# Opening of a fused transformer kernel: two value units multiplied before the shift is known

## The reference, cut to what matters

```python
ada = jax.nn.silu(c) @ w_ada[l] + b_ada[l]
sh1, sc1, g1, sh2, sc2, g2 = [a[:, None, :] for a in jnp.split(ada, 6, axis=-1)]
h = x * (1.0 + sc1) + sh1
qa, ka, va, qb, kb, vb = jnp.split(h @ w_in, AB_SPLITS, axis=-1)
```

## Time and profile before

| | |
|---|---|
| median of 3 runs | 1231.37 us |
| the profiled execution | 1228.85 us |
| its span | 1227.2 us |
| PE busy | 1188.8 us (97%) |
| DVE busy | 673.6 us (55%) |
| ACT busy | 503.5 us (41%) |
| chain that ended last | PE 79%, DVE 8%, DMA 8%, ACT 3% |
| DMA in the first 31 us (the first of 40 slices) | 370 GB/s |

### The profile page before, as it was taken

The page is one execution under the profiler, slowest core; times in us unless marked ns, Lnnn a source line. Parts: engine busy times, 40 slices in busy tenths (PEclk is TensorE's granted clock), DMA queues, the critical chain, the costliest instruction groups (busy, mean ns, idle before and its releaser), DMA issues.

```text
span 1227.2 us, 16442 instructions
## 1 busy us (share of the span) xinstructions
PE 1188.8 (97%) x6522; PEld 816.1 (66%) x6522; DVE 673.6 (55%) x1206; ACT 503.5 (41%) x779; POOL 53.6 (4%) x103
## 2 busy tenths in 40 slices
PE   6999999999999999999999999999999999999997
PEld 2697688888889878888878786455444444544436
DVE  5689979887889787864476685112111111111126
ACT  1579563434565576344448384111111111111125
POOL 0100001000010000010001100000000000000000
PEclk9999999999999999999999999999999999999999
DMA  9996868888846555856567779999999999999991
GB/s 370 391 350 269 315 235 323 333 311 300 315 162 244 187 214 202 304 192 216 186 234 247 265 309 415 418 425 423 426 425 428 424 426 425 427 423 426 425 421 43
DMA packets 50987, 394.98 MB, mean 322 GB/s; under 512 B 6673, under 2 KB 8913, under 8 KB 11378
## 3 DMA queue, kind: packets, MB, share of 16 engines
q1 hardware_dynamic: 39618, 337.18, 68.6%
q0 software_dynamic: 9072, 53.92, 12.3%
q10 hardware_dynamic: 2240, 3.10, 0.9%
HBM read 390.68 MB, written 3.49 MB: 321 GB/s over the span
## 4 chain that ended last, share of the span: by engine, by line
PE 79%; DVE 8%; DMA 8%; ACT 3%; issue 1%; SPq 1%; DVEq 0%; ACTq 0%
PE psum L1400 16%; PE psum L770 10%; PE psum L773 10%; PE psum L777 10%; PE psum L1443 7%; DMA slabs<-in_w 5%; PE psum L1332 4%; PE psum L843 2%; PE psum L847 2%; PE psum L845 2%; DMA staged<-in_ada 2%; PE psum L1340 2%; DVE w_parts L2151 2%; PE psum L1095 1%; PE psum L1107 1%; PE psum L1086 1%
## 5 line engine op out<-in xcount | busy, mean ns | idle before, releaser
L2151 DVE TENSOR_TENSOR w_parts<-w_raw,w_parts 128x2048 fp32r<-128x2048 f32 x106 | 241.7, 2287 | 62.4 <-ACT w_parts L1533 62.3
L1533 ACT ACTIVATE w_parts<-w_raw 128x2048 fp32r<-128x2048 f32 x106 | 202.0, 1911 | 70.6 <-DMA w_raw<-in_units 70.5
L1400 PE MATMUL psum<-slabs,arena 128*64 128x512 f32 x768 | 223.2, 593 | 2.4 <-DMA w_odd_late<-in_w 1.8
L770 PE MATMUL psum<-w_parts,h_parts 128*128 128x512 f32 x392 | 155.2, 396 | 3.7 <-ACT h_parts L1533 1.9
L773 PE MATMUL psum<-w_parts,h_parts 128*128 128x512 f32 x392 | 153.0, 390 | 0.0
L1533 ACT ACTIVATE arena<-psum 128x512 f32<-128x512 f32 (+1 forms) x59 | 29.9, 509 | 295.3 <-PE psum L1419 141.7
L1400 PEld LDWEIGHTS psum<-slabs,arena 128*64 128x64 f32 x768 | 71.3, 137 | 112.7 <-issue 106.8
L777 PE MATMUL psum<-w_parts,h_parts 128*128 128x512 f32 x392 | 105.3, 390 | 0.6 <-DVE h_parts L2329 0.6
L2134 DVE CUSTOM_DVE_ANT_0 aring<-aring,cb 128x1024 f32<-128x1024 f32 x80 | 94.5, 1218 | 1.2 <-DMA aring<-in_ada 1.2
L770 PEld LDWEIGHTS psum<-w_parts,h_parts 128*128 128x128 f32 x392 | 73.6, 188 | 20.3 <-issue 2.9
L1400 PE MATMUL psum<-w_odd,arena 128*64 128x512 f32 x192 | 85.1, 593 | 0.4 <-DMA slabs<-in_w 0.4
(11 more groups left out here) (338 smaller groups left out, 1932.1 us busy)
## 6 DMA issues: line engine op xcount, KB each, us to landing
w_raw<-in_units SPq DMA_DIRECT2D x110, 1024.0 KB, 5.0
slabs<-in_w SPq DMA_DIRECT2D x52, 1024.0 KB, 15.4
slabs<-in_w SPq DMA_DIRECT2D x22, 2048.0 KB, 21.7
aring<-in_ada POOLq DMA_DIRECT2D x40, 1024.0 KB, 5.6
arena<-in_w SPq DMA_DIRECT2D x16, 2048.0 KB, 20.7
w_odd<-in_w SPq DMA_DIRECT2D x16, 2048.0 KB, 19.8
w_odd<-in_w SPq DMA_DIRECT2D x24, 1024.0 KB, 25.5
staged<-in_ada SPq DMA_DIRECT2D x8, 1024.0 KB, 18.7
```

The source lines that it names most:

```text
L770: mm(psum[:, bank, :], high(tile, tok), w_hi(k)[:, col:col + 512], start=first and bank not in begun, stop=False, skip_group_check=True)
L1400: ins = nc.tensor.matmul(psum[s * CAP:(s + 1) * CAP, w, :], xe_t[:, kt, s * CAP:(s + 1) * CAP], up_weights(w, s, b, kt), start=kt == 0, st ...
L1533: return nc.scalar.activation(out_ap, in_ap, func, **kw)
L2151: v.tensor_tensor(w_lo(k), raw(k), w_hi(k).bitcast(F32), ALU.subtract).then_inc(w_split, 1)
```

## The change

The order of the conditioning pieces becomes 4, 5, 6, 2, 7, 3, 0, 1: the scales of kt 0 to 3 first, then scale and shift of kt 4 to 7, and the shifts of kt 0 to 3 last (`LATE_SHIFT` = 4). Units 0 and 1 are multiplied with `x * scale` alone. Their missing part is made when the shifts are there: `shift_products` multiplies the shift, copied to 32 columns, with units 0 and 1, one tile of features on each quarter of the array's columns, into PSUM banks 4 and 5; ACT and DVE split that into two rounded parts (`shift_rows`), and `shift_sums` adds the parts to the four value banks through a matrix of ones. The other half of `h` (`h_hi`, `h_lo` of kt 0 to 3) is made late too (`shifted_h`, `first_low`), from `x_first` with the shift as a bias.

Query/key unit 4 is worked on in two halves of its tiles (`first_heads`): kt 4 to 7 before the shift products, kt 0 to 3 behind them. It and unit 5 write to PSUM banks 6 and 7 instead of 0 and 1. Units 0 and 1 lie in buffers of their own (`w1_odd`, `v_second`), since they are needed until the end of the opening. Some semaphores take over a second use, with their later counts raised.

The diff, without the semaphores' second uses:

```diff
@@ -82,9 +82,10 @@
 RMS = ("mix", "ple_proj", "ffn", "gate", "final")
 GAINS = ("g_mix", "g_ple_proj", "g_ffn", "g_ple", "g_final")
 
-CONSTS, LATER = 2 * 16, 6 * 16
-
-ADA_ORDER = (4, 0, 5, 1, 6, 2, 7, 3) + tuple(range(8, 48))
+CONSTS, LATER = 2 * 16, 5 * 16
+
+ADA_ORDER = (4, 5, 6, 2, 7, 3, 0, 1) + tuple(range(8, 48))
+LATE_SHIFT = 4
 STAGED = 8
 ADA_PIECES = 48
 
...
@@ -282,6 +283,10 @@
 
         w2_at = [arena[:], at("w2_odd", 0, [P, 8192])[:]]
 
+        first_v = [w1_odd[:], at("v_second", 178, [P, UNIT])[:]]
+        shift_rows = at("shift_rows", 136, [P, 2, 2, 512], F32R)
+        shift_ones = at("shift_ones", 144, [P, P], F32R)
+
         def slab(which, s, b):
 
...
@@ -531,18 +544,31 @@
-            for i in range(4):
-                stage(2 * i)
-                if i < 3:
-                    tiles = slice(2 * i, 2 * i + 2 if i < 2 else KT)
-                    sp.dma_start(x_first[:, tiles, :], a["x_t"][:, tiles, :]).then_inc(staged_in[2 * i + 1], 16)
-                stage(2 * i + 1)
-                load_unit(i)
+            stage(0)
+            sp.dma_start(x_first[:, 0:2, :], a["x_t"][:, 0:2, :]).then_inc(x_first_in[0], 16)
+            load_unit(0)
+            stage(1)
+            sp.dma_start(x_first[:, 2:4, :], a["x_t"][:, 2:4, :]).then_inc(x_first_in[1], 16)
+            load_unit(1)
+            stage(2)
+            stage(3)
+            sp.dma_start(x_first[:, 4:KT, :], a["x_t"][:, 4:KT, :]).then_inc(x_first_in[2], 16)
+            load_unit(2)
+            stage(4)
+            stage(5)
+            load_unit(3)
             load_unit(4)
...
-            small_loads(((lam_in[:], a["lam_in"]), (bias[:, 16, :], a["causal"]), (w_forget[:], a["w_forget"]),
+            stage(6)
+            stage(7)
+            load_unit(5)
+            load_unit(6)
+            sp.dma_start(lam_in[:], a["lam_in"]).then_inc(lam_arrived, 16)
+            load_unit(7)
...
@@ -694,6 +720,7 @@
 
 
             pool.wait_ge(bias_copied, 16)
+            pool.wait_ge(w_loaded[0], 32)
             bands(0, 4)
             pieces(8, 22)
             pool.wait_ge(unit_done, WO_AT + 4)
...
@@ -802,11 +829,55 @@
                         for c in range(2):
                             col = 1024 * s + 512 * c
                             ins = mm(psum[:, 2 * t + c, :], x_first[:, 2 * i + s, t * P:(t + 1) * P],
-                                     raw(V_AT + i)[:, col:col + 512], start=i == 0 and s == 0, stop=i == 3 and s == 1,
+                                     raw(V_AT + i)[:, col:col + 512], start=i == 0 and s == 0, stop=False,
                                      skip_group_check=True)
-                    if i == 3 and t == 0:
-                        ins.then_inc(v_half, 1)
                 ins.then_inc(unit_done, 1)
+
+            def first_heads(tiles):
+
+                k = QK_AT
+                begins, ends = tiles[0] == LATE_SHIFT, tiles[-1] == LATE_SHIFT - 1
+                made = lambda kt: (kt - LATE_SHIFT) % KT + 1
+                at_ = lambda kt, s: slice(kt * 256 + s * P, kt * 256 + (s + 1) * P)
+                pe.wait_ge(w_hi_ready, split_no(k))
+                for n, kt in enumerate(tiles):
+                    pe.wait_ge(h_high, made(kt))
+                    for s in range(2):
+                        mm(half(6, s), w_hi(k)[:, at_(kt, s)], h_hi[:, kt, :], start=begins and n == 0 and s == 0, stop=False,
+                           skip_group_check=True)
+                for kt in tiles:
+                    pe.wait_ge(h_low, made(kt))
+                    for s in range(2):
+                        mm(half(6, s), w_hi(k)[:, at_(kt, s)], h_lo[:, kt, :], start=False, stop=False, skip_group_check=True)
+                weights(k)
+                for kt in tiles:
+                    for s in range(2):
+                        ins = mm(half(6, s), w_lo(k)[:, at_(kt, s)], h_hi[:, kt, :], start=False,
+                                 stop=ends and kt == tiles[-1], skip_group_check=True)
+                if ends:
+                    ins.then_inc(unit_done, 1)
+
+            def shift_products():
+
+                pe.wait_ge(ada_done, STAGED)
+                for c in range(2):
+                    for kt in range(LATE_SHIFT):
+                        ins = mm(psum[32 * kt:32 * kt + 32, 4 + c, :], ada[:, 0, kt:kt + 1].to_broadcast([P, 32]),
+                                 raw(V_AT + kt // 2)[:, kt % 2 * 1024 + c * 512:kt % 2 * 1024 + c * 512 + 512],
+                                 start=True, stop=True, skip_group_check=True)
+                    ins.then_inc(shift_mm, 1)
+
+            def shift_sums():
+
+                pe.wait_ge(shift_high, 2)
+                for t in range(TT):
+                    for c in range(2):
+                        for part in range(2):
+                            if part and t == 0:
+                                pe.wait_ge(shift_low, shift_low_from + c + 1)
+                            ins = mm(psum[:, 2 * t + c, :], shift_ones[:], shift_rows[:, part, c, :], start=False, stop=part == 1,
+                                     skip_group_check=True)
+                    ins.then_inc(v_half, 1)
 
             def to_values(i, t):
                 return from_h(LAYER_UNITS + V_AT + i, i // 2, t, 2 * t + i % 2, 1)
...
@@ -1184,6 +1258,10 @@
                 if layer == 0:
                     for i in range(4):
                         first_values(i)
+                    first_heads((4, 5, 6, 7))
+                    shift_products()
+                    first_heads((0, 1, 2, 3))
+                    shift_sums()
                     pe.wait_ge(consts_in, CONSTS)
                 else:
                     to_values(0, 0)
...
@@ -1567,7 +1645,15 @@
             act.wait_ge(rows_mm, 1)
             A(cb[:], psum[:, 5:7, :].rearrange("p c n -> p (c n)"), ACT.Silu).then_inc(silu_c, 1)
 
+            def first_scaled(p):
+                act.wait_ge(x_first_in[p], 16)
+                act.wait_ge(scale_ready, p + 1)
+                for kt in (2 * p, 2 * p + 1):
+
+                    A(x_first[:, kt, :], x_first[:, kt, :], Cp, scale=small[:, kt:kt + 1]).then_inc(h_first, 1)
+
...
+            def shifted_h(p):
+                act.wait_ge(ada_done, 7 + p)
+                for kt in (2 * p, 2 * p + 1):
+                    act.wait_ge(h_first, kt + 1)
+                    A(h_hi[:, kt, :], x_first[:, kt, :], Id, bias=ada[:, 0, kt:kt + 1]).then_inc(h_high, 1)
+
+            first_scaled(0)
+            for dst, src in ((cst[:], a["consts"]), (added_in[:], a["added"])):
+                act.dma_start(dst, src).then_inc(consts_in, 16)
+            first_scaled(1)
+            act.wait_ge(bias_row, 1)
+            act.dma_start(scratch, added_in[:].unsqueeze(1).to_broadcast([16, COPIES, 384])).then_inc(bias_copied, 16)
+            first_h(2)
+            first_h(3)
+            act.wait_ge(consts_in, CONSTS)
+            act.wait_ge(ada_done, 5)
+            A(shift_ones[:], ones, Cp)
             split(4)
+            shifted_h(0)
+            shifted_h(1)
+            for c in range(2):
+                act.wait_ge(shift_mm, c + 1)
+                A(shift_rows[:, 0, c, :], psum[:, 4 + c, :], Cp, scale=1.0 / 32).then_inc(shift_high, 1)
+            split(5)
 
...
             def first_low(p):
                 for kt in (2 * p, 2 * p + 1):
-                    dve.wait_ge(h_high, kt + 1)
-                    v.tensor_tensor(h_lo[:, kt, :], x_first[:, kt, :], h_hi[:, kt, :].bitcast(F32),
-                                    ALU.subtract).then_inc(h_low, 1)
...
+                    dve.wait_ge(h_high, (kt - LATE_SHIFT) % KT + 1)
+                    if kt < LATE_SHIFT:
+                        stt(h_lo[:, kt, :], x_first[:, kt, :], ada[:, 0, kt:kt + 1], h_hi[:, kt, :].bitcast(F32),
+                            ALU.add, ALU.subtract).then_inc(h_low, 1)
+                    else:
+                        v.tensor_tensor(h_lo[:, kt, :], x_first[:, kt, :], h_hi[:, kt, :].bitcast(F32),
+                                        ALU.subtract).then_inc(h_low, 1)
+
+            piece(0)
+            first_scale(0, 1)
+            piece(1)
+            first_scale(1, 2)
+            dve.wait_ge(consts_in, CONSTS)
+            dve.wait_ge(rows_mm, 2)
+            stt(added_in[:], psum[0:16, 4, 0:384], -1.0, added_in[:], ALU.mult, ALU.add).then_inc(bias_row, 1)
+            pieces(2, 4)
+            first_scale(2, 4)
+            pieces(4, 6)
+            first_scale(3, 6)
+            first_low(2)
             first_low(3)
             split(4)
+            piece(6)
+            first_low(0)
+            piece(7)
+            first_low(1)
+            for c in range(2):
+                dve.wait_ge(shift_high, c + 1)
+                stt(shift_rows[:, 1, c, :], psum[:, 4 + c, :], 1.0 / 32, shift_rows[:, 0, c, :].bitcast(F32), ALU.mult,
+                    ALU.subtract).then_inc(shift_low, 1)
             split(5)
```

(22 more changed lines are left out.)

59 lines of the change are left out of this document (25 added, 34 removed).

## The result

| | before | changed |
|---|---|---|
| median of 14 runs each, us | 1230.28 (1228.07 to 1233.18) | 1232.75 (1230.67 to 1234.33) |
| ratio, 95% interval | | 1.0019 [1.001, 1.0028] |
| profiled execution, us | 1228.85 | 1232.55 |
| its span, us | 1227.2 | 1230.8 |
| TensorE clock granted over it | 0.999 | 0.997 |

The ratio is +2.3 us (1.2 to 3.4).

The account below looks back on a forecast made before the run. Opening bound by loads, then PE, whose start on unit 5 decides. Values 5.8 us earlier, less 2.85 idle, 1.9 products, 1.8 sums: +0.8; ring 0.2 more: +1.0, 1232.4 us; 8 in 10 from 1228.3 to 1237.0.

Parts of the forecast that it names:

- Loads: Opening, SP's queue: unit 4 lands at 37.3 us, the last two conditioning buffers at about 40 and 42.6.
- Values: Opening, PE: value products start at 10.8 instead of 14.28 and end at 42.1, 5.8 us earlier than 47.93.
- The wait: PE, ahead of the shift products: idle from 45.0 to 47.85, 2.85 us, for DVE's pieces behind unit 4's split.
- The shift products: PE, after the last shift piece: they run side by side on column quarters and take 1.9 us, to 49.75.
- Second half and sums: PE, before unit 5: second half of unit 4 takes 2.88 us, the eight shift sums 1.8.
- two chains end together: At unit 5's start: PE is free and DVE's split of unit 5 ends, both at 54.5 us.
- One to one: Behind the opening: a shift of PE's start on unit 5 reaches the kernel's end in full.
- The ring: DVE's ninth piece: ring load issued 5 us later, DVE waits 0 to 3.2 us; 0.2 us added, ends 0 and 2.
- The first rival (late ring): Late first ring load at DVE's ninth piece is handed down: sum +5.8, 1237.2 us; chance 0.17.
- Serial products: Opening, PE: shift products run one behind another, 7.10 us instead of 1.9; +6.0, 1237.4 us; chance 0.05.
- A shorter chain: Opening, DVE: chain shorter than reckoned, PE's idle falls to 0; sum -1.9 or -3.1, 1228.3 us; chance 0.15.
- The fourth, no change: Opening: PE and not the shift is what follows, 5.8 us won and given back; 0.0, 1231.4 us; chance 0.18.

Follow-up runs that it names:

- s1: Changed kernel with each shift product on all 128 columns, one after another; median 1236.02 us, ratio to before 1.0054.
- s4: Changed kernel with buffer 6 loaded and pieces 6, 7 done before unit 4's split, and unit 7's split ahead of DVE's ninth piece; 1229.73 us, ratio 0.9997.
- s8: Changed kernel run and profiled once more, no edit; 1230.97 us, span 1229.1.
- s7: Kernel before the change, run and profiled once more, no edit; 1230.62 us, span 1228.9.
- s3: Changed kernel with buffer 6 loaded ahead of unit 4, pieces 6 and 7 ahead of its split, PE's unit 4 products reordered; 1229.69 us, ratio 0.9992.
- s9: Same kernel as s4, timed once more beside the changed kernel; 1229.36 us, ratio to before 0.999.
- s5: Changed kernel with POOL waiting for the load of unit 7 instead of unit 5; one run, 1233.86 us.
- s2: Changed kernel without POOL's wait for unit 5's load, so its bands start earlier; 1232.5 us, ratio 1.0023.
- s6: Changed kernel without shift products, shift rows and shift sums, so values lack the shift of four tiles; 1230.0 us, ratio 1.0.
- s10: Changed kernel, no edit, timed and profiled again; 1231.92 us against 1229.88 before, ratio 1.0016.

## Why the prediction was right, and what it sized too small

Forecast: unit 5 +0.8, in all +1.0 (1232.4 by the median then shown). Measured: +2.3 (1.2 to 3.4) by the ratio, 1.9 in like profiles. The mechanism held; the size was half of what came. That 1232.4 and 1232.75 lie so close is partly luck: the kernel before had 1231.37 in the three runs shown and 1230.28 in fourteen.

- **Loads.** Right. Unit 4 was forecast to land at 37.3; ACT's wait for it ended at 37.46. DVE waited for neither of the last two pieces' transfers.
- **Values.** Right, with one term optimistic. Start 10.90 (forecast 10.8), unit 0 to 20.1 (20.0), unit 1 to 27.0 (27.1), unit 2 to 34.0 (34.2). The first unit's products started 0.85 us apart up to 15.3 and 0.43 apart from 15.8 on, which makes some 2 us more, as forecast. The forecast speaks of a warm array for the later ones; the granted clock reads 1.00 from 10 to 20 us, and no run shows what slows the first. Unit 3 began at 35.94, not 35.0: DVE waited for both buffers of its round, and the later one came only at 32.32 (forecast 31.8); the rest is ACT's scaling. The gain of the values was thus 4.9, not 5.8. It cost nothing: PE would have waited for the last piece by as much more.
- **The wait.** Right. Forecast 2.85 of idle from 45.0 to 47.85; 2.28 to 48.19. The chain began 0.25 later than reckoned (41.70 for 41.45) and its hand-over was longer: I took 0.38 for each rest and 0.45 for ACT, and there were 0.89 for both and 0.54. The two pieces themselves took 2.52 and 2.54 for 2.6 each. In sum +0.34.
- **The shift products.** Right: 1.92 (forecast 1.9), 3.7 times quicker than in full columns (7.15 in s1). The 0.4 that the forecast's range holds for the products is a term that no run shows; what the runs show in its place is 1.92, that is 0.02 above the forecast.
- **Second half and sums.** Mis-sized. 3.07 for 2.88 (the first 8 products, right behind the shift products, took 1.15 instead of 0.96, for a reason that no run shows) and 1.84 for 1.8: +0.23. That two chains end together was right: DVE's split of unit 5 ran from 52.60 for 2.29 us, to 0.15 ahead of PE's start.
- **Reading of the start.** These make 55.04 instead of 54.5 (54.43 before rounding). I compared with 53.69, a start in the chain's view, which counts from the end of the product ahead. The timeline has the same product start at 53.52, and from 53.52 to 55.04 it is +1.52. Its first scores come 8.80 later in the changed kernel and in s1 to s4, 8.73 in the one before. That makes +1.59, where the first scores were found.
- **One to one.** Right for delays, shown by s1: +5.11 at unit 5, +5.1 at the end. For the change itself, like with like, 1.84 at the first scores became 1.9 at the end (s8 against before) and 1.7 became 1.9 (the first profile against s7). A gain is handed on less fully: in s3 and s9 the span is 0.9 and 0.4 longer, against like profiles of before, than their first scores say, in s4 0.1. What takes this away has no shown cause; the clock is not it, as the like profiles have the same number of falls.
- **The ring.** The term of 0.2 was not needed: 0.64 of waiting, well inside the forecast 0 to 3.2, and no wait of PE for unit 7 behind it. The first rival (late ring) falls with it, by s5 above all: 6.8 us later still, and 0.80 of waiting (one profile). In s3, where DVE came 2 us earlier, the wait was 2.85.
- **The other rivals.** Serial products: refuted by the starts 0.01 apart and by s1. A shorter chain, and so a faster kernel: the chain was not shorter, the addition of the last piece starts at 47.97. s3 and s4 show what that rival would have been worth: unit 5 at 52.7 to 52.9, and the time of before or a little under. The fourth, no change, lies just outside of the intervals.
- **Not in the prediction at all:** the clock. The gaps that the change makes in the opening are followed by a lower clock in some executions. The kernels that idle there for over 2 us (the change three times, s1, s2, s5, s6) had a granted clock of 0.58 to 0.73 behind it in three of seven profiles (s5 0.58 and s10 0.61 from 48 to 52 us, s6 0.73 from 56 to 60); those that don't (before twice, s3, s4, s9) in none of five. It costs 1.4 to 1.5 us when it comes (in s10 from the first shift product to unit 5 8.28 us instead of 6.85, in s6 from unit 5 to the first scores 10.28 instead of 8.80). The length of the gap alone does not decide it: ahead of the last value unit, at 36 us, PE idles 1.06 to 2.46 us in the ten profiles of the change and its variants, and the granted clock stays at 1.00 behind it in all of them.
- **How often the clock falls.** The executions for which a mean clock is on record, most of them without a profile, speak for the same. The clock granted over a whole execution is on the average 0.9964 in 27 of the change, 0.9961 in ten of s2 and 0.9967 in ten of s6, but 0.9976 in 66 of the kernel before and in 35 of s3, s4 and s9 together; one fall is worth 0.0014. How much of the time goes with it stays open. Three of seven times 1.5 would be 0.6 on the average, enough for the step from 1.9 in like profiles to the 2.3 and 2.0 of the two ratios. Nearly one more fall in each execution, as the mean clocks say, would be more than that step holds, and s1, which has the gap too, has 0.998 in its four.

## What to carry to other kernels

When an engine is fed earlier, write down in order everything that its feeder must do before each piece it hands over: here the split of unit 4, which PE needed anyway, stood ahead of the two pieces PE waited for, and cost 2.3 us of a gain of 4.9, which left too little to pay the 3.8 of the new products. Small work put in that order first, and work that waits for nobody behind it, was worth 2.2 us without removing one instruction. When two starts are compared across kernels, take both from the same view.

## What the runs showed of the hardware

- The granted clock of TensorE fell from 1.00 to 0.50 (slices of 1 us) in some executions and not in others of the same kernel, behind 0.35 or 0.36 us of idle at the gathering products (five of twelve profiles) and in the opening in three of the seven profiles with over 2 us of idle there. Each fall took 1.7 us of full clock away: 32 gathering products took 3.84 us in seven profiles and 5.46 or 5.47 in five, with the same idle ahead of them in the four profiles shown (0.35 or 0.36 us). One profile of each of the two kernels differed by 1.63 us in this way, which the second pair of profiles (s7, s8) had the other way round.
- Of the fp32 shift products of 512 columns, each on 32 of the array's columns, four started nearly together and the next four 0.43 to 0.45 us later (48.19, 48.64, 49.07, 49.50); on all columns, in s1, it was 0.45 for each. The 16 records took 1.92 us against 7.15.
- The bands, moved earlier on POOL's queue in s2, delayed loads of SP's queue: without POOL's wait the engines moved 298 instead of 418 GB/s from 38 to 46 us, DVE waited 0.39 us for the last piece of the opening and 2.41 us for `lam_in`.
